# A decoder step with a paged sample group: the selected keys gathered row by row in place of all past keys under a mask

## What is computed

```
def dsa_sample(qa, ka, va, qi, ki, wi, cache_k, cache_v, cache_ik, page_table, bias_a):
    ...
    ki_all = jnp.concatenate([gather_pages(cache_ik, page_table).astype(ki.dtype), ki], axis=1)
    idx, valid = select_keys(indexer_scores(qi, wi, ki_all), qpos, n_keys, min(TOPK_MAX, n_keys // 4))
    k_sel = gather_selected(cache_k, page_table, ka, idx, past)
    v_sel = gather_selected(cache_v, page_table, va, idx, past)
    return dsa_core(qa, k_sel, v_sel, valid, qpos[None, :, None] - idx, bias_a)
```

## Time and profile before

| | us |
|---|---|
| median of 3 runs | 2460.18 |
| lowest and highest | 2459.58 and 2466.08 |
| the profiled execution, span | 2590.7 |
| start to the first gather of group B's keys in it | 596.6 |
| group B, 32 units | 596.6 to 1150 |
| group A's past keys and new tokens | 1150 to 1335.2 |
| feed-forward and down projection | 1755 to 2590.7 |

### The profile page before, as it was taken

How to read it: one execution, slowest core, us unless ns; L and a number is a source line. 1 busy time by engine, 2 the same in 40 slices (tenths; PEclk the granted TensorE clock), 3 DMA queues, 4 the chain that set the end, 5 groups by cost and what they waited for, 6 DMA issues and landing times. The chain is left out here.

```text
span 2590.7 us, 32530 instructions
## 1 busy us (share of the span) xinstructions
PE 2312.3 (89%) x12169; PEld 1549.6 (60%) x12189; DVE 1103.6 (43%) x2687; ACT 766.2 (30%) x2065; POOL 660.5 (25%) x703
## 2 busy tenths in 40 slices
PE   7999997767777878788789898899999999999999
PEld 5644443443455455555444445548888888888887
DVE  5489998742445533333322212352443343371001
ACT  3551345653444444444421013311111111110000
POOL 1451223123544445433301010013222121201110
PEclk9999998988889889998889999999999999999999
DMA  4211101025888778765540014111111111122221
GB/s 140 73 60 70 38 9 65 1 82 188 275 277 269 234 266 281 257 213 193 173 162 28 33 49 163 34 67 34 50 34 50 34 50 40 44 65 74 74 63 39
DMA packets 147603, 281.75 MB, mean 109 GB/s; under 512 B 13479, under 2 KB 82775, under 8 KB 147447
## 3 DMA queue, kind: packets, MB, share of 16 engines
q0 software_dynamic: 48384, 176.18, 20.2%
q1 hardware_dynamic: 80774, 90.50, 10.6%
q10 hardware_dynamic: 18288, 12.98, 1.7%
HBM read 261.68 MB, written 17.94 MB: 108 GB/s over the span
## 5 line engine op out<-in xcount | busy, mean ns | idle before, releaser
L634 PE MATMUL PS<-region 128*128 128x512 f32 (+5 forms) x864 | 327.7, 534 | 1.8 <-DMA region<-w_in 1.8
L2784 PE MATMUL PS<-region,ffn_w 128*128 128x264 f32 x1408 | 323.1, 388 | 1.6 <-PEq L2234 1.6
L2784 PEld LDWEIGHTS PS<-region,ffn_w 128*128 128x128 f32 x1408 | 269.2, 191 | 48.4 <-issue 1.9
L2004 ACT COPY region<-PS 128x512 f32<-128x512 f32 x352 | 197.2, 591 | 212.6 <-PE PS L1868 72.2
L634 PEld LDWEIGHTS PS<-region 128*128 128x128 f32 (+1 forms) x864 | 152.7, 181 | 161.2 <-issue 140.9
L2784 PE MATMUL PS<-region,side 128*128 128x264 f32 x1056 | 245.0, 389 | 1.8 <-POOL side L2741 1.8
L1875 PE MATMUL PS<-ident_f,region 128*128 128x128 f32 x1024 | 170.7, 316 | 82.4 <-ACT region L2004 44.1
L2784 PEld LDWEIGHTS PS<-region,side 128*128 128x128 f32 x1056 | 200.0, 191 | 35.8 <-POOL side L2741 1.9
L1875 PEld LDWEIGHTS PS<-ident_f,region 128*128 128x128 f32 x1024 | 133.5, 162 | 117.0 <-issue 76.3
L931 DVE TENSOR_SCALAR_CACHE_REDUCE mask<-score,cand 128x384 bf16<-128x384 f32 (+2 forms) x198 | 180.9, 942 | 3.4
L1109 POOL DMA_INDIRECT region<-cache_b_k,gather_b x128 | 120.4, 941 | 212.0 <-PE PS L1875 177.8
(11 more groups left out here) (448 smaller groups left out, 4017.7 us busy)
## 6 DMA issues: line engine op xcount, KB each, us to landing
ffn_w<-w_gate SPq DMA_DIRECT2D x11, 1024.0 KB, 5.4
ffn_w<-w_up SPq DMA_DIRECT2D x11, 1024.0 KB, 5.5
region<-w_in SPq DMA_DIRECT2D x4, 2048.0 KB, 7.9
ffn_w<-w_down ACTq DMA_DIRECT2D x7, 704.0 KB, 5.6
region<-x_prompt ACTq DMA_DIRECT2D x8, 512.0 KB, 7.1
region<-x_prompt SPq DMA_DIRECT2D x8, 512.0 KB, 10.6
mem_keys<-cache_mem_k SPq DMA_DIRECT2D x8, 512.0 KB, 5.0
mem_values<-cache_mem_v SPq DMA_DIRECT2D x8, 512.0 KB, 8.0
```

What stands on the lines that cost most here:

```text
L634: last = nc.tensor.matmul(M.PS[0:n, s % 3, 0:chunks[j].width], XT[:, c, t * P:t * P + n], w[j % 2][:, c, 0:chunks[j].width], start=(c == 0 ...
L2004: nc.scalar.copy(dst, M.PS[0:dst.shape[0], T0 + x % 2, 0:dst.shape[1]]).then_inc(t_read, 1)
L2784: last = nc.tensor.matmul(M.PS[:, bank, 0:TW], left[:, c, :], right[:, c, :], start=begin and c == 0, stop=(c == KH - 1), skip_group_check ...
```

## The change

Group B's walk is kept. Of group A's 18 chunks, six stay: for each g two chunks of 512 listed keys and one "near" chunk, which holds the last page of each sequence (its 128 keys have a position bias of their own and are treated under the mask as before) and the new tokens.

Behind the binary search 41 steps z write the list. Step z0 puts the cache row number of each position into the kept places of `work`, and zero elsewhere. Steps z1 to z32 each take the eight largest numbers of a row with one MAX and wipe them with one MATCH_REPLACE. Steps z33 to z38 shift the four segments' lists behind one another by powers of two, z39 adds them up on PE, z40 turns the list into an index table `ids` and a short mask. No step z but z34 and z39 uses PE or ACT. Three steps c or z stand in each chunk from chunk 0 on, where there were two c, so c ends in chunk 10 and z runs from chunk 11 to chunk 24.

The gathers of group A change from 64 of 512 KB to 16 of 64 KB for the last pages (`near`) and 128 of 64 KB for the listed rows (`chosen`): four sets (one a chunk) of 16 for keys and 16 for values. `near` is issued behind units 26 and 27, set 0 behind units 28 to 31, eight gathers behind each unit; sets 1, 2 and 3 follow. The cost of the prompt's steps in `beside` changes too: c counts half, z nothing, all others one.

```diff
-        cut = iter(range(33))
+        cut = iter([("c", r) for r in range(33)] + [("z", r) for r in range(self.LISTED + 1)])
         for n in range(end + 1):
             keys = [("k", n + 1, j) for j in range(1 if self.new(n + 1) else 4)] if n < end else []
-            self.steps += keys[:3] + [("p", n)] + keys[3:] + [("o", n)] + [("c", r) for r in itertools.islice(cut, 1)]
+            self.steps += keys[:3] + [("p", n)] + list(itertools.islice(cut, 1)) + keys[3:] + [("o", n)]
+            self.steps += list(itertools.islice(cut, 1))
             if n < end:
-                self.steps += [("s", n + 1)] + [("c", r) for r in itertools.islice(cut, 1)]
+                self.steps += [("s", n + 1)] + list(itertools.islice(cut, 1))
...
+        def near(b):
+            gather(near_k[:, b, :], near_loaded, kv_rows["A", 0], M.gather_n, b)
+            gather(near_v[:, b, :], near_loaded, kv_rows["A", 1], M.gather_n, b)
+
+        def chosen(x, v, j):
+            out, arrived = (set_values_at(x, j), set_values[x]) if v else (set_keys_at(x, j), set_keys[x])
+            for q in range(4):
+                t, half = 2 * (x % 2) + q // 2, q % 2
+                gather(out[:, q * P:(q + 1) * P], arrived, kv_rows["A", v], ids,
+                       half * NS + DEC_T * (4 * (x // 2) + j) + t)
...
+        for u in range(1, walk.n_units):
+            keys(u)
             values(u)
+            if u == last - 5:
+                eng.wait_ge(listed, 2)
+            if last - 5 <= u < last - 3:
+                for b in range(4 * (u - last + 5), 4 * (u - last + 5) + 4):
+                    near(b)
+            if last - 3 <= u <= last:
+                for j in range(2 * ((u - last + 3) % 2), 2 * ((u - last + 3) % 2) + 2):
+                    chosen(0, (u - last + 3) // 2, j)
+        used(last - 2)
+        for v in range(2):
+            for j in range(4):
+                chosen(1, v, j)
+        for j in range(4):
+            turned(last, j)
+            chosen(2, 0, j)
+        for j in range(4):
+            chosen(2, 1, j)
+        used(last)
+        for v in range(2):
+            for j in range(4):
+                chosen(3, v, j)
...
+            elif r <= walk.ROUNDS:
+                eight = lists[0][:, 8 * (r - 1):8 * r]
+                link(nc.vector.max(eight, work[:, 0:SEGW]))
+                link(nc.vector.match_replace(work[:, 0:SEGW], eight, work[:, 0:SEGW], 0.0))
```

More of the change, by code:

```diff
@@ L1523, in selective_and_sample_stage @@
         walk, pool_part, sync_part, s_pe, s_act, s_dve = sample_attention(nc, io, M, K, S)
-        selective = [n for n, (kind, g, c) in enumerate(walk.chunks) if kind == "A"]
-        order = beside(walk.steps, a_steps,
-                       lambda step: 0.5 if step[0] in "kspof" and step[1] in selective else 1.0, lambda step: 1.0)
+        order = beside(walk.steps, a_steps, lambda step: {"c": 0.5, "z": 0.0}.get(step[0], 1.0), lambda step: 1.0)
         def run(sample, selective):
@@ L1589, in __init__ @@
         self.news = [n for n in range(end + 1) if self.new(n)]
[L1590 to L1592 removed]
+        self.n_units = sum(kind == "B" and c >= 0 for kind, g, c in self.chunks)
+        self.units = [n for n, (kind, g, c) in enumerate(self.chunks) if kind == "B" and c >= 0]
+        self.sets = [n for n, (kind, g, c) in enumerate(self.chunks) if kind == "A" and c >= 0]
         self.fill, x = {}, 0
@@ L1604, in new, with near @@
         return self.chunks[n][2] < 0
+    def near(self, n):
+        return self.new(n) and self.chunks[n][0] == "A"
     def first(self, n):
@@ L1609, in width, with keys_arrivals, values_arrivals, last_turned @@
     def width(self, n):
[L1610 to L1618, removed]
-    def aside(self, u):
[L1622 to L1644, removed]
+        if self.new(n):
+            return P + NS if self.near(n) else NS
+        return P * RKB if self.chunks[n][0] == "B" else CH
+    def aside(self, u):
+        return u % 2 == 1 and u < self.n_units - 1
+    def keys_arrivals(self, u):
+        return NCI + u + 1
+    def values_arrivals(self, u):
+        return (u + 1) // 2 if self.aside(u) else NCI + (u + 1) // 2 + 1
     def rescaled(self, n):
         return sum(not self.first(m) for m in range(n))
+    def last_turned(self, n):
+        return self.fill["k", n, 0, 0] if self.near(n) else self.fill["k", n, 3, 1 if self.chunks[n][0] == "B" else 0]
     def fills(self, step):
@@ L1653, in fills @@
             return [x + (j,) for x in self.index if self.turned_at(x) == step for j in range(4)]
-        if step[0] == "k" and not self.new(step[1]):
+        if step[0] == "k" and (not self.new(step[1]) or self.near(step[1])):
             return [step + (x,) for x in range(2 if self.chunks[step[1]][0] == "B" else 1)]
+        if step[0] == "z":
+            return [step] if step[1] in (self.ROUNDS + 2, self.ROUNDS + 7) else []
         return [step] if step[0] in "pc" else []
@@ L1882, in logits @@
             out = M.PS[:, L0, 0:w]
-            if not walk.new(n):
-                eng.wait_ge(t_read, fill["k", n, 3, 1 if kind == "B" else 0] + 1)
+            if not walk.new(n) or walk.near(n):
+                eng.wait_ge(t_read, walk.last_turned(n) + 1)
             if n:
@@ L1961, in outputs, with list_kept @@
             last.then_inc(pv_done, 1)
+        def list_kept(step):
+            if step not in fill:
+                return
+            if step[1] == walk.ROUNDS + 2:
+                eng.wait_ge(counted_kept, 1)
+                t = bank(step)
+                nc.tensor.matmul(t[:, 0:1], K("seg_before"), count[:, 0:1], start=True, stop=True).then_inc(t_full, 1)
+                return
+            eng.wait_ge(shifted, 1)
+            t = bank(step)
+            for half in range(2):
+                nc.tensor.matmul(t[:, half * NS:(half + 1) * NS], lists[0][:, half * P:(half + 1) * P],
+                                 K("seg_sum")[:, 0:NS], start=half == 0, stop=True, skip_group_check=half > 0)
+            nc.tensor.matmul(t[0:NS, 2 * NS:2 * NS + TOPK], K("seg_sum")[:, 0:NS], lists[0], start=False, stop=True,
+                             skip_group_check=True).then_inc(t_full, 1)
         for g in range(2):
@@ L3295, in build @@
         M.gathered = [ctx.enter_context(nc.semaphore(f"gathered{i}")) for i in range(8)]
+        M.near_loaded = ctx.enter_context(nc.semaphore("near_loaded"))
+        M.set_keys, M.set_values = ([ctx.enter_context(nc.semaphore(f"set_{n}{x}")) for x in range(4)]
+                                    for n in ("keys", "values"))
         M.mem_loaded = ctx.enter_context(nc.semaphore("mem_loaded"))
```

279 lines of the change are left out of this document (188 added, 91 removed).

## The result

The changed kernel takes **2505.87 us** (median of 4 runs, 2503.75 to 2510.47) against 2463.03 us of the kernel before on the same chip (4 runs): a ratio of 1.018 [1.015, 1.021], 1.8% slower. 2442 us had been forecast, with a range up to 2490.

The account below looks back on a forecast made before the run. Group B was taken to go at its own gathers' rate, with POOL's row setting the pace from unit 26. Profiled, -44 + 11 + 3 + 1 = -29 us; for the runs, the middle of -27 and -9, -18, gave 2442 us, range 2412 to 2490.

Parts of the forecast that it names:

- baseline: Kernel before: group B takes 16.1 us a unit; the 130.5 us between span and runs spread evenly over 1755 us.
- The old path: Kernel before, from POOL's first gather for unit 26's keys to the stage's end: 311.9 us profiled, 289 in the runs.
- The new path: Changed kernel, same stretch: POOL's row of 192 gathers with two waits 249 us, landing 2, PE's remaining order 17.
- the pitch that stays: Behind unit 26, POOL's 1.24 us a gather does not shrink in unprofiled runs: new path 280 us, change gives -9 us.
- PE mostly idle behind group B: Sign that the prediction is right: PE mostly idle in the stretch after group B; no size given.
- The list: Chunks 11 to 24, DVE: MAX and MATCH_REPLACE 1.28 us each, 32 rounds 85 us, mostly beside other work; +11 us, ends 0 and 44.
- The cover: PE's wait for keys, 2.7 to 4.0 us a chunk, hides the maximum being 1.7 us late in most chunks.
- DVE's rounds come on the path: Slower rival: two of three rounds a chunk precede something PE needs; 3 us more in 11 chunks, 2473 us; chance 0.16.
- The gain is eaten: No-change rival: POOL's pitch stays and the early shift is 24 us rather than 15; 2460 us; chance 0.20.
- The steps c: Chunks 0 to 10: three steps c a chunk instead of two, DVE has room; +3 us, ends 0 and 10.
- Small gathers dear: Slower rival: POOL's 144 small gathers take 1.5 us each, 37 us more; 2476 us; chance 0.08.
- POOL held: Slower rival: DVE's rounds hold up POOL's gathers, 2.6 us a chunk in 11 chunks; 2468 us; chance 0.04.

Follow-up runs that it names:

- first profile: The kernel before, unchanged, in the profiled execution that the prediction read; some 130 us above the median of that kernel's unprofiled runs.
- second profile: The kernel before, unchanged, profiled a second time; 2460.97 us, span 2459.2 us.

## Why the prediction was wrong, point by point

- **The failed step is the baseline.** The prediction read "So group B goes at the rate of its own gathers: 32 units in 515 us, 16.1 us a unit", and spread the 130.5 us between the span and the runs evenly over 1755 us. Both rest on an execution in which this one stage ran 132 us longer. The rows were read rightly, but that the 130.5 us might lie in one stage was not looked at. In an ordinary execution a unit takes 13.0 us, and the waits that were to cover the new work are mostly gone.
- **The old path.** From unit 26's keys to the end the first profile has "311.9 us", which the prediction scaled to 289; the second profile has 268.1. The new path, "249 + 2 + 17 = 268", measured 275.6 with the two products of the norm that the 17 us include. Its parts nearly hold: a pitch of 1.25 us from one gather to the next; 12.64 us of waiting ahead of unit 31's values (9, ends 4 and 14; a gather of 512 KB for group B's keys took 6.1 us to land at the median, where some 4 had been taken for four of them); 20.1 us from the last gather's start to the end (19). So a gain of 44 us (or of 9 with the pitch that stays) became a loss of 6.2 (7.5 with those two products), because the old path was sized from the first profile. "PE mostly idle behind group B" came half true: from 1120 us to the end of the stage PE is busy 65.9 of 132 us.
- **The list.** The instructions were priced well: 1.22, and 0.09 + 1.21 us, against 1.28 each. The cover was not: "PE's wait for keys in the same place, 2.7 to 4.0 us, covers that in most chunks". Six chunks had 16.6 us of such waits in the first profile and 3.3 in the second. The rounds cost 26.7 us where 11 was taken, with an end of 44. The rival "DVE's rounds come on the path" had the mechanism, its place, and the point from which it decides (1.8 us a chunk; it came to 2.4 in 11 chunks), and was given 0.16.
- **Two rivals came together.** "The gain is eaten" (POOL has taken over as what group A waits for) and the rounds on the path were priced as alternatives. They are independent, as the runs with half the gathers show, and their sum, with the old path at 268, is outside the range.
- **The steps c, and the prompt's steps.** +3 us were forecast in chunks 0 to 10; it was 13.0. The run with three steps c alone has 12.2 of this and gives all of it back in the chunks that then have none. In the changed kernel that gain isn't seen: from chunk 10 to unit 26 it takes 185.5 us without rounds against 168.0 in the kernel before with three steps c. What fills those 17.5 us is not separated. Step z0 and the last eight steps of the list stand there, and 49 of the prompt's steps instead of 45. The weights in `beside`, which the change sets anew, have no term in the prediction's sum. That such weights matter is shown: with 16 prompt steps fewer ahead of unit 26, its keys came 20.1 us sooner, 5.3 of them by chunk 10 and 14.8 from there on.
- **Small gathers dear, POOL held.** Neither came: 944 ns for 64 KB against 937 for 512 KB, and 104.60 against 104.53 us of POOL with and without rounds. The Trainium skill, "SBUF — State Buffer", section "Who interferes with whom", says that a DVE instruction with at most one SBUF input, outside the two-port modes, does not contend with GpSimd; the rounds behave so here.
- **The sum by measured terms** is 13.0 + 31.6 + 6.2 = 50.8 us for the stage, and 49.0 in the spans. The medians differ by 42.8 us, with an interval of 38 to 51; the changed kernel's profiled execution took 2510.47 us, 4.6 more than its median. Of the 31.6 us, 26.7 are the rounds.

## What to carry to other kernels

Before a profiled time is used as a baseline, lay it against the unprofiled runs, and where they differ find the stage that holds the difference: idle time there is no cover for new work. Replacing bytes by instructions pays only where bytes end the waits; here 64 gathers of 512 KB became 144 of 64 KB at the same 1.25 us each, and the change paid only with less of the prompt's work beside group B (25 us, the largest single step) and with a row on POOL that started earlier. Two slow mechanisms in different stretches add up, so price them together and not as alternatives.

## What was not expected of the hardware

- Two profiled executions of one program differed by 132 us in one stage and by almost nothing elsewhere: 256 to 261 GB/s against 316 to 330, with a granted clock of 0.88 against 0.97 to 0.99. Why the first was slow is open.
- A gather of 128 rows takes 0.94 to 0.95 us of POOL and begins 1.25 us behind the last, with 512 bytes, 1 KB or 4 KB a row.
- A round of 2.57 us on DVE cost 0.8 us with three of them spread over a chunk, and the 32 rounds some 24 us more in all when the three stood together, on a DVE that was idle a quarter of the time.
